# Output projections as seven half-size products, with the weight sums made during the merge

## The reference, cut to what matters

```python
def first_block(x, ...):
    ...
    branch = jnp.einsum('nbsw,nwd->nbsd', ys, w_branch[layer])
    gates = jax.nn.sigmoid(gate_logits.reshape(b, s, N_BRANCH, D_MODEL)...)
    merged = jnp.einsum('bsnd,nbsd->bsd', gates, branch)
    x = x + merged @ w_out[layer]

def second_block(x, ...):
    ...
    merged = g_a * (y_pool @ w_proj_pool[l]) + g_b * (y_nsa @ w_proj_nsa[l])
    x = x + merged @ w_out[l]
    h = rms_norm_2(x, norm_mlp[l])
    x = x + jnp.square(jax.nn.relu(h @ w_ff1[l])) @ w_ff2[l]
    return rms_norm_2(x, norm_final)
```

## Time and profile before

| what | value |
|---|---|
| median of three runs | 1474.15 us |
| the profiled execution's own time | 1473.68 us |
| its span, first to last instruction | 1471.7 us |
| TensorE busy | 1433.2 us, 97% |
| VectorE busy | 790.6 us, 54% |
| ScalarE busy | 648.4 us, 44% |
| GpSimd busy | 618.0 us, 42% |
| DMA, mean | 89 GB/s |
| matmuls | 7741 |

### The profile page before, as it was taken

One profiled execution on the slowest core, in us unless ns is written; L12 is line 12 of the kernel. 1 busy time (PEld: TensorE's weight loads), 2 busy tenths in 40 slices (PEclk: granted clock), 3 DMA queues, 4 the chain that ended last, 5 costly groups with the idle time before them and its releaser, 6 DMA issues.

```text
span 1471.7 us, 20985 instructions
## 1 busy us (share of the span) xinstructions
PE 1433.2 (97%) x7741; PEld 1198.0 (81%) x7741; DVE 790.6 (54%) x1566; ACT 648.4 (44%) x1164; POOL 618.0 (42%) x437
## 2 busy tenths in 40 slices
PE   8999999989989999999999999999999899999998
PEld 7888888768778888889997777788888788888886
DVE  4336958466663041421234777762222777777776
ACT  5453644558563222342234566763324433223342
POOL 4333645344343444434343355553444513333330
PEclk9999999999999999999999999999999999999999
DMA  6222532203002333436432110004323423333321
GB/s 205 82 82 83 154 95 83 63 14 99 31 1 58 100 101 99 146 114 197 138 104 72 58 30 2 2 2 157 101 100 92 137 89 110 102 100 100 100 86 57
DMA packets 73049, 130.44 MB, mean 89 GB/s; under 512 B 5815, under 2 KB 29954, under 8 KB 72962
## 3 DMA queue, kind: packets, MB, share of 16 engines
q1 hardware_dynamic: 71682, 126.04, 27.9%
q10 hardware_dynamic: 1280, 3.22, 0.6%
HBM read 125.05 MB, written 4.19 MB: 88 GB/s over the span
## 4 chain that ended last, share of the span: by engine, by line
PE 92%; DVE 3%; ACT 2%; issue 1%; POOL 1%; DMA 1%; POOLq 0%; SPq 0%; DVEq 0%; ACTq 0%
PE bank L946 63%; PE bank L1605 9%; PE bank L1177 4%; PE bank L1185 4%; PE bank L1008 4%; PE bank L875 3%; PE bank L906 1%; PE bank L1010 1%; PE bank L1593 1%; PE bank L1421 0%; DVE item_lo L3041 0%; PE bank L1128 0%; DMA proj<-in_x 0%; DVE prob_t L2626 0%; DVE q_parts L2510 0%
## 5 line engine op out<-in xcount | busy, mean ns | idle before, releaser
L720 POOL TENSOR_TENSOR w_lo<-raw,w_hi 128x1024 fp32r<-128x1024 f32 (+3 forms) x189 | 441.7, 2343 | 507.2 <-ACT w_hi L1681 507.0
L1681 ACT ACTIVATE w_hi<-raw 128x1024 fp32r<-128x1024 f32 (+3 forms) x193 | 195.5, 1016 | 438.4 <-DMA raw<-in_w_in 214.2
L946 PE MATMUL bank<-w_hi,xt_hi 128*128 128x484 f32 (+2 forms) x648 | 242.3, 374 | 0.0
L946 PE MATMUL bank<-w_hi,xt_lo 128*128 128x484 f32 (+2 forms) x648 | 240.0, 370 | 0.0
L946 PE MATMUL bank<-w_lo,xt_hi 128*128 128x484 f32 (+2 forms) x648 | 240.0, 370 | 0.0
L946 PE MATMUL bank<-xt_hi,w_hi 128*128 128x512 f32 x560 | 221.3, 395 | 0.0
L946 PE MATMUL bank<-xt_hi,w_lo 128*128 128x512 f32 x560 | 218.2, 390 | 0.0
L946 PE MATMUL bank<-xt_lo,w_hi 128*128 128x512 f32 x560 | 218.1, 389 | 0.0
L946 PEld LDWEIGHTS bank<-w_hi,xt_hi 128*128 128x128 f32 x648 | 121.7, 188 | 15.4 <-issue 0.6
L946 PEld LDWEIGHTS bank<-w_hi,xt_lo 128*128 128x128 f32 x648 | 121.6, 188 | 15.3
L946 PEld LDWEIGHTS bank<-w_lo,xt_hi 128*128 128x128 f32 x648 | 121.8, 188 | 14.4
(11 more groups left out here) (416 smaller groups left out, 2690.0 us busy)
## 6 DMA issues: line engine op xcount, KB each, us to landing
raw<-in_w_in SPq DMA_DIRECT2D x40, 512.0 KB, 3.6
raw<-in_w_in SPq DMA_DIRECT2D x40, 484.0 KB, 3.5
raw<-in_w_ff SPq DMA_DIRECT2D x36, 512.0 KB, 3.7
quarter_b<-in_w_ff SPq DMA_DIRECT2D x28, 512.0 KB, 3.5
raw<-in_w_in SPq DMA_DIRECT2D x24, 392.0 KB, 3.4
raw<-in_w_out SPq DMA_DIRECT2D x16, 512.0 KB, 3.5
raw<-in_w_branch SPq DMA_DIRECT2D x12, 512.0 KB, 3.6
raw<-in_w_mem_kv SPq DMA_DIRECT2D x8, 512.0 KB, 3.6
```

What stands on the lines that cost most here:

```text
L720: pool.tensor_tensor(w_lo[:, slot, 0:halves, 0:width], raw[:, slot, 0:halves, 0:width], w_hi[:, slot, 0:halves, 0:width].bitcast(F32), ALU ...
L946: ins = pe.matmul(o, lhs, rhs, start=st and j == 0, stop=en and j == 2)
L1681: act.activation(w_hi[:, slot, 0:halves, 0:width], raw[:, slot, 0:halves, 0:width], ACT.Copy)\
```

## The change

The output projections use Winograd's form as the feed-forward part does: `out_products` runs seven products of 256 tokens by 512 rows by 512 columns, 24 matmuls each, two weight pairs each, so 14 pairs of 12 matmuls for 8 pairs of 24. Four products need sums of weight quarters, four need sums of merged rows.

Weight sums: while the second and third branch are merged, SP loads eight chunks (four for each `w_out`, 1 MB each in two DMAs), VectorE makes the sums (`sum_chunk`, four operations), and SP stores them whole to DRAM (`sums_d`). `out_weights` loads quarters from there or from `w_out`, and they are rounded and split like any pair. Row sums: `sum_rows` on VectorE after each half of `merged_lo`, their high halves by ScalarE (`sum_hi`), their low parts by VectorE (`sum_lo`). The load of x moves ahead of the roundings of pairs 0 and 1 on ScalarE. At the feed-forward start the first weight sums go ahead of the wait for r_kept, `weights_lo` behind `rows_lo`, and the last two quarters are loaded in the other order.

```diff
+OUT_PRODUCTS = (1, 7, 4, 6, 2, 5, 3)
+OUT_BANK = {1: 0, 7: 2, 4: 6, 6: 4, 2: 0, 5: 4, 3: 4}
+S_ORDER = (7, 6, 5, 3)
...
+            def chunk_load(c):
+                k, kt, w = c % 2, c % 4, (w_out, w_out_2)[c // 4]
+                if c < 2:
+                    sp.wait_ge(sem["emptied_d"], strips_emptied("D", STRIP_MERGE + 3))
+                else:
+                    sp.wait_ge(sem[f"chunk_out{k}"], 32 * (c // 2))
...
+            def chunk_store(c):
+                k, kt = c % 2, c % 4
+                sp.wait_ge(sem["chunk_summed"], 3 * c + 3)
...
+            def side_transfers(j):
+                if j >= 7 and j % 2 == 1 and (j - 7) // 2 < 8:
+                    chunk_store((j - 7) // 2)
+                if j >= 4 and j % 2 == 0 and (j - 4) // 2 < 8:
+                    chunk_load((j - 4) // 2)
...
+            def out_products(n, s, p0):
+                a_hi, a_lo = xt
+                for i, m in enumerate(OUT_PRODUCTS):
+                    if m == 1:
+                        free_banks(0, lambda j: s)
+                    if m == 4:
+                        free_banks(0, lambda j: s + 1)
+                    if m in (2, 5, 3):
+                        pe.wait_ge(sem["out_added"], 7 * n + {2: 1, 5: 4, 3: 6}[m])
+                    if m in S_ORDER:
+                        pe.wait_ge(sem["sums_hi"], 4 * n + S_ORDER.index(m) + 1)
+                        pe.wait_ge(sem["sums_lo"], 4 * n + S_ORDER.index(m) + 1)
...
+                    for q in range(2):
+                        p = p0 + 2 * i + q
+                        wait_pair(p)
+                        if m in (1, 4):
+                            pe.wait_ge(sem["mhi"], 4 * n + (m == 4) * 2 + q + 1)
+                            pe.wait_ge(sem["mlo"], 4 * n + (m == 4) * 2 + q + 1)
...
+                    if m == 5:
+                        for k in range(4):
+                            turn_x(n + 1, k)
...
+            for k in range(2):
+                act.wait_ge(sem[f"chunk_out{k}"], 128)
+            act.wait_ge(sem["ys_lo"], 2)
+            act.dma_start(proj[:, 0:TT, XRES:XRES + D], x[0]...)
             for q in range(2):
                 next_hi(PAIR_OUT1 + q, S)
+            def sum_hi(n, k):
+                act.wait_ge(sem["row_sums"], 4 * n + (1, 3, 3, 4)[k])
+                act.mul(row_sum_hi[n][k], row_sum[n][k]..., 0.5).then_inc(sem["sums_hi"], 1)
+            def merged_hi(n, src):
+                for t in range(TT):
+                    act.wait_ge(sem["merged_in"], 2 * n + t // 2 + 1)
+                    act.mul(xt_hi[:, 2 * t:2 * t + 2, :], src(t), 0.5).then_inc(sem["mhi"], 1)
+                    if t == 1:
+                        sum_hi(n, 0)
+                        for q in (2, 3):
+                            next_hi((PAIR_OUT1, PAIR_OUT2)[n] + q, S)
+                for k in range(1, 4):
+                    sum_hi(n, k)
+                    next_hi((PAIR_OUT1, PAIR_OUT2)[n] + 3 + k, S)
...
             def raw_hi(n, v, p_out, p_next, width, scratch):
+                for q in range(7, 13):
+                    next_hi(p_out + q, S)
+                squares(n, 0, scratch)
+                next_hi(p_out + 13, S)
...
+            for q in range(2):
                 next_hi(PAIR_OUT2 + q, S)
...
+            def sum_rows(n, part):
...
+                if part == 0:
...
+                    dve.tensor_tensor(s3, a11, a21, ALU.subtract).then_inc(sem["row_sums"], 1)
+                    sum_lo(n, 0)
+                    return
+                dve.tensor_tensor(s1, a21, a22, ALU.add).then_inc(sem["row_sums"], 1)
+                dve.wait_ge(sem["row_sums"], 4 * n + 2)
+                dve.tensor_tensor(s2, s1, a11, ALU.subtract).then_inc(sem["row_sums"], 1)
+                dve.wait_ge(sem["row_sums"], 4 * n + 3)
+                dve.tensor_tensor(s4, a12, s2, ALU.subtract).then_inc(sem["row_sums"], 1)
+                for k in range(1, 4):
+                    sum_lo(n, k)
...
             for b in range(2):
                 weigh(STRIP_M2 + 6 + b, False, GATED2, None)
                 merged_lo(None, 1, b)
+                sum_rows(1, b)
...
                 rows_lo(i, t)
-                if not isinstance(i, int):
-                    weights_lo(i, t)
+                weights_lo(i, t)
...
+            weight_sums(0, lambda j: 0)
             dve.wait_ge(sem["r_kept"], 1)
             dve.tensor_tensor(r_squared[:], r_rows[:], r_rows[:], ALU.mult).then_inc(sem["r_squared"], 1)
             dve.wait_ge(sem["r_squared"], 1)
-            weight_sums(0, lambda j: 0)
-            weights_lo(0, lambda j: 0)
```

More of the change, by code:

```diff
@@ L284, in two_block_kernel @@
         part_sums = [place(f"part_sum{k}", [P, 2, S], where=E - 4096 + 1024 * k) for k in range(3)]
+        chunk = [place(f"chunk{k}", [P, 4, S], where=E - 4096 + 2048 * k)[:] for k in range(2)]
+        m_sums = place("m_sums", [P, 4, D], where=E - 4096)
+        m_sums_lo = place("m_sums_lo", [P, 4, D], F32R, where=E - 4096)
+        row_sum = [[v.rearrange("p (a b n) -> p a b n", a=2, b=2) for v in of]
+                   for of in ([m_sums[:, k, :] for k in range(4)], [proj[:, k, 2560:3584] for k in range(4)])]
+        row_sum_lo = [[v.rearrange("p (a n) -> p a n", a=4) for v in of]
+                      for of in ([m_sums_lo[:, k, :] for k in range(4)], [projr[:, k, 2560:3584] for k in range(4)])]
+        row_sum_hi = [[projr[:, k, c:c + D].rearrange("p (a n) -> p a n", a=4) for k in range(4)] for c in (GATED, 1536)]
+        sums_d = [nc.dram_tensor(f"sums{n}", (D, D), F32, kind="Internal").ap() for n in range(2)]
         h_last = (xt_hi[:, 0:TT, :], xt_lo[:, 0:TT, :])
@@ L808, in _ @@
             attention("b")
-            split_run(PAIR_MERGE + 12, PAIR_IN2, S)
+            split_run(PAIR_MERGE + 12, PAIR_OUT1 + 12, S)
+            for p in range(PAIR_OUT1 + 12, PAIR_IN2):
+                split(p, p % RING, 2, S)
             split_run(PAIR_IN2, PAIR_IN2 + 4, IN2_W)
@@ L816, in _ @@
             attention("n")
-            split_run(PAIR_M2 + 16, PAIR_FF, S)
+            split_run(PAIR_M2 + 16, PAIR_OUT2 + 12, S)
+            for p in range(PAIR_OUT2 + 12, PAIR_FF):
+                split(p, p % RING, 2, S)
             split_run(PAIR_FF, PAIR_FF + 4, S)
@@ L1396, in _ @@
                 merge(n, ys[n % 2] if n else ys_a)
-            for b in range(2):
-                strip(0, lambda j: STRIP_OUT1 + b, lambda j: PAIR_OUT1 + 4 * b, 4, xt, S, False,
-                      before=merged_then_turn(0) if b else merged_parts(0))
+            out_products(0, STRIP_OUT1, PAIR_OUT1)
             def key_columns(kt):
@@ L1572, in _ @@
                 strip(0, lambda j: STRIP_M2 + 6 + b, lambda j: m2 + 20 + 4 * b, 4, (yn_hi, yn_lo), S, True)
-            for b in range(2):
-                strip(0, lambda j: STRIP_OUT2 + b, lambda j: PAIR_OUT2 + 4 * b, 4, xt, S, False,
-                      before=merged_then_turn(1) if b else merged_parts(1))
+            out_products(1, STRIP_OUT2, PAIR_OUT2)
             def ff_up(f, s, p, before=None):
@@ L2072, in merge_act @@
             def merge_act(n):
[L2074 to L2076 removed]
+                for j in range(12):
+                    next_hi(PAIR_MERGE + 12 * n + j, S)
+                    if j == 7:
                         gate1_tanh(STRIP_MERGE + 4 * n, gated1(0))
[L2078 removed]
                 gate1_tanh(STRIP_MERGE + 4 * n + 1, gated1(1))
```

169 lines of the change are left out of this document (112 added, 57 removed).

## The result

The changed kernel takes 1481.84 us (median; 1481.58 to 1483.82), the kernel before 1474.15: ratio 1.0056, 95% interval 1.0044 to 1.0068, so 7.7 us slower. The forecast was 1482.8. The profiled execution took 1481.58 us with a span of 1479.7, 8.0 more than the span before.

The account below looks back on a forecast made before the run. TensorE, busy 97% of the span, was taken to bound the kernel. First projection +8.4, second +7.0 and feed-forward start -6.5 gave +8.9 us on 1473.68 or the median 1474.15: forecast 1482.8 us, range 1475 to 1488.

Parts of the forecast that it names:

- part 1: Output projections: 24 matmuls fewer in each, saving 4.8 us per projection, 9.6 together.
- The walk: Operation times worked through in order around both projections; the first ends at 655.9 (+8.4 us), the second at 1131.0 (+7.0).
- The term for the clock: Behind the wait in each projection TensorE's clock falls to half, costing 2.4 us.
- Rival 1: Smaller stalls in the projections: no exclusion of VectorE and GpSimd, or no clock fall; 1471 to 1479 us, chance 0.17.
- Now the order on ScalarE decides: First projection: ScalarE rounds pair 4 only after a row-sum half that waits for s2; pair ready at 624.0.
- part 4: Row sums between merge and products make TensorE wait 10.1 and 9.3 us; projections +8.4 and +7.0 us.
- theory A: Forecast of an experiment: with pair 4 rounded early, both projections' waits and slow clock go, about -17 us, to 1465.
- rival 2: Projections: pair 4 isn't late, so the change does what its counts say; 1458 us, chance 0.10.
- Part 2: Six more weight pairs per projection: 7.4 us from freed slot to ready pair, covered by 8.3; cost zero.
- Part 3: Weight sums during the merge: 16 MB more DMA and 32 VectorE additions, covered; cost zero, 0 to 2 us.
- Part 5: Feed-forward start: the 3.9 us wait and 2.6 us of slow clock go, -6.5 us.
- slower still: Loads 1.5 us longer, a pair each 2.92 us in the projections, feed-forward wait may stay; 1486 to 1492 us, chance 0.11.

Follow-up runs that it names:

- e3b: Changed kernel with pairs 4 and 5 rounded ahead of the late row sums and half-width GpSimd splits in both projections, weights' low part left out; 1465.79 us.
- the run with the filler: Changed kernel with 36 matmuls of no use put ahead of product 4 in each output projection; 1480.42 us.
- e1: Changed kernel with only ScalarE's order altered: pairs 4 and 5 rounded ahead of the three later row sums; 1480.47 us.
- e9: Changed kernel with pairs 4 and 5 rounded early and the low parts of the last three row sums of each projection left out; 1478.12 us.
- the two runs: Feed-forward edits alone in the kernel before, 1468.37 us; the same edits taken out of the changed kernel, 1489.30 us.
- the four cells above: Changed kernel, pair 4 rounded late or early, splits whole or half: late whole 1481.84, early whole 1480.47, late half 1474.46, early half 1465.79 us.

## Why the prediction was right, and where it wasn't

- **The sum.** +8.9 forecast, +8.0 in the spans and +7.7 in the medians. Its terms were 8.4, 7.0 and -6.5; measured are 8.8, 5.7 and -6.5. That the total is only 1 us off is in part luck: the first projection was put 0.4 too low and the second 1.3 too high.
- **The gain of seven products** (part 1). 24 matmuls fewer in each projection, as said, and TensorE 8.4 us less busy over the span. In e3b, with both limits lifted, 2.6 of the 9.6 us come out as time.
- **The wait in the first projection.** Forecast 10.1 us from 613.9 to 624.0, measured 9.59 before 624.51, released by GpSimd's split of pair 4. End forecast 655.9, measured 656.36. The walk had the second pair 1.5 us late from the x load; in fact pair 0 was late too (ScalarE waits 7.59 us for its load and rounds it at 594.87, where the kernel before rounded its pair 0 at 589.65). The walk had no wait in front of pair 2, where TensorE waits 1.31 us: that pair is rounded at 605.35, behind the half of s3, and s3 stands behind the xt_lo that two splits stretched to 5.08 us.
- **The second projection.** Forecast +7.0, measured +5.7: the wait was 8.79 instead of 9.3, and 96 matmuls behind it took 23.83 us, where the first projection took 24.57. The term for the clock, 2.4 us each, was sized by the earlier trace rows; the run with the filler shows that it mostly stood in the place of another limit, the pace of the pairs: 1.1 and 0.3 us came back. The sum was right with it, but the name was wrong. Rival 1 had said that without a fall of the clock GpSimd's splits would be late and the gain only 2 us, and so it was (1.4).
- **"Now the order on ScalarE decides"** (part 4) is the sentence that fell. The order puts the wait where it is, but with pair 4 early it was worth 1.4 us and not the 17 that theory A of e1 made of the two waits and their slow clock. The prediction's rival 2 (pair 4 not late, 1458) left out that the splits and VectorE's work, and the exclusion between them, which part 4 had counted with 3.8 and 4.0 us, also hold back what comes behind. The numbers were right since the walk had the exclusion in it; the reason was half of it.
- **Part 2** took the supply as 7.4 us by loads, rounding and a split of 2.33. The split runs at that pace only when VectorE is not at it: 2.36 in e9, 2.78 in e1.
- **Part 3**: the merge holds no wait of TensorE, as forecast.
- **Part 5**: -6.5 forecast, -5.6 to -6 measured in the two runs. Within the trace of the changed kernel (+14.5 at the end of the second projection, +8.0 after the first 84 products) it is -6.5.
- **The rivals.** The gain didn't come; "slower still" (a supply of 2.92 us per pair, a feed-forward wait that stays) neither. Its mechanism, a supply that falls short of TensorE, was there, at GpSimd and not at the loads.

What stays open: the split of the remaining loss between the stretched chain in front of product 4 and the order, since the two limits can't be added (the four cells above); and how much of the second limit is GpSimd's own 33.6 us of splits and how much the exclusion, for the half splits shorten both and the run without the low parts moved the time by little. Weight sums kept in DRAM already rounded and split, which would take 8 of the 14 splits out, weren't tried.

## What to carry to other kernels

A product saved on the busiest engine can be worth nothing if the remaining ones need more from the engines that feed it: here a projection went from 8 splits in 45.3 us to 14 in 40.5. Before such a change, add up for the stage not each engine by itself but those together that exclude each other. Here that sum was an estimate, and the runs bear it out in direction rather than in size. When the wait that you name has been removed and the time stays, look at the releasers of the new waits, and lift the second limit together with the first.

An edit bundled with others should be timed alone: the feed-forward part was worth 6 us by itself, and the rest of the change lost 13.5 (1481.84 against 1468.37).

## What the runs showed of the hardware

- The price of the exclusion, for the same operations: four additions with two SBUF operands 2.50 us alone, 4.52 beside one split, 6.74 beside two; two low parts 5.99 in the changed kernel (1.22 each when undisturbed). GpSimd's split: 2.36 to 2.41 alone, 2.78 on the mean with VectorE's low parts in between. VectorE's four products that read a PSUM bank beside a split (606.62, split of 606.47) took 2.47 us, as without one (2.48 at 591.50).
- A TensorE kept at work in its wait by 36 useless matmuls keeps its granted clock at 1.00; standing for 9.6 us it was at 0.50 when it began again and back at 1.00 some 5 us later. That only 1.4 us of 4.8 came back with the clock was the surprise.
